# Order of the head of a hybrid decoder layer: constants and x first, gate2's sum around tile 1's first norm, its projection during the first routing, output weights scaled between slots

## The reference

```python
mod = silu(c) @ w_ada + b_ada
shift1, scale1, gate1, shift2, scale2, gate2 = split(mod, 6)
h = rms_norm(x, g_norm1) * (1 + scale1) + shift1
a, u, v = split(h @ w_in)                       # 512 columns each
mixed = concat([pool_mixer(a, w_pool, pool_scale), spatial_gating(u, v, ...)])
x = x + gate1 * (mixed @ w_out)
h = rms_norm(x, g_norm2) * (1 + scale2) + shift2
# for each token and head: two sets of 128 scores, top 16 of each, top 16 of the 256 sums
q = (h @ w_query).reshape(T, 8, 2, 128); scores = einsum(q, sub_keys)
idx, gate = top16 of the sums, softmax of their values
act = gelu(einsum('thkd,td->thk', expert_down[idx], h))
y = einsum('thk,thkd->td', gate * act, expert_up[idx])
return rms_norm(x + gate2 * y, g_final)
```

## Time and profile before

| | us |
|---|---|
| median of 3 runs | 2980.74 (2976.18 to 2981.69) |
| the profiled execution's own time | 2976.63 |
| its span, first to last instruction | 2974.8 |
| first gather issued | 158.9 |
| first expert sum on PE (slot 0) | 192.9 |
| DVE busy in the span | 1914.0 |
| PE busy in the span | 1978.3 |
| share of POOL's queue in the DMA engines' span | 88.2% |

### The profile page before, as it was taken

The page is one execution under the profiler, slowest core; times in us unless marked ns, Lnnn a source line. Parts: engine busy times, 40 slices in busy tenths (PEclk is TensorE's granted clock), DMA queues, the critical chain, the costliest instruction groups (busy, mean ns, idle before and its releaser), DMA issues.

```text
span 2974.8 us, 37539 instructions
## 1 busy us (share of the span) xinstructions
PE 1978.3 (67%) x12770; PEld 903.2 (30%) x12770; DVE 1914.0 (64%) x4705; ACT 1208.4 (41%) x3855; POOL 1150.8 (39%) x1032
## 2 busy tenths in 40 slices
PE   4579887887877466666656756666766666565553
PEld 3354452543543223222222322222322223222110
DVE  5666766576765476667576776667576766667544
ACT  1125454454453343444334443444334444344333
POOL 0033333334334244444444443444444444444332
PEclk9789987988988556675666556666566656666555
DMA  9469999999999999999999999999999999999997
GB/s 406 174 258 411 378 414 358 380 409 401 410 390 385 409 409 420 421 410 421 421 420 421 410 421 421 414 410 420 417 421 419 409 410 421 421 403 417 418 421 294
DMA packets 176213, 1181.83 MB, mean 397 GB/s; under 512 B 19731, under 2 KB 28947, under 8 KB 42774
## 3 DMA queue, kind: packets, MB, share of 16 engines
q0 software_dynamic: 147456, 1073.81, 88.2%
q1 hardware_dynamic: 28566, 105.63, 9.1%
HBM read 1170.98 MB, written 8.39 MB: 396 GB/s over the span
## 4 chain that ended last, share of the span: by engine, by line
DMA 54%; PE 23%; DVE 12%; ACT 6%; issue 3%; SPq 1%; POOL 0%; DVEq 0%; ACTq 0%; POOLq 0%
DMA work<-experts,expert_rows 39%; DMA weights<-experts,expert_rows 11%; PE ps_sum L746 7%; DVE work L1285 5%; PE ps_m L664 4%; PE ps_small L715 3%; PE ps_wide L690 2%; PE ps_m L608 2%; PE ps_m L628 2%; ACT diag L929 1%; ACT weight L924 1%; PE ps_m L619 1%; DMA out<-h_next 1%; DVE weights L1285 1%; DMA x_buf<-x 1%
## 5 line engine op out<-in xcount | busy, mean ns | idle before, releaser
L560 POOL DMA_INDIRECT work<-experts,expert_rows x832 | 928.3, 1116 | 1493.5 <-PE ps_sum L746 1311.7
L1285 DVE CUSTOM_DVE_ANT_0 work<-work 128x1024 f32<-128x1024 f32 x832 | 1015.0, 1222 | 658.0 <-DMA work<-experts,expert_rows 656.7
L746 PE MATMUL ps_sum<-work,diag 128*32 128x256 f32 x6656 | 745.4, 533 | 671.5 <-ACT diag L929 669.4
L922 ACT ACTIVATE act_out<-act_in 128x1 f32<-128x1 f32 x1024 | 207.4, 202 | 1206.7 <-DVE act_in L1285 1204.0
L746 PEld LDWEIGHTS ps_sum<-work,diag 128*32 128x32 f32 x6656 | 153.6, 127 | 1154.4 <-ACT diag L929 1086.0
L929 ACT ACTIVATE diag<-const,weight 128x32 f32<-128x32 f32 x1024 | 329.1, 321 | 33.5
L1285 DVE CUSTOM_DVE_ANT_0 weights<-weights,work 128x1024 f32<-128x1024 f32 x192 | 234.8, 1223 | 158.6 <-DMA weights<-experts,expert_rows 158.0
L560 POOL DMA_INDIRECT weights<-experts,expert_rows x192 | 219.5, 1143 | 299.2 <-PE ps_sum L746 281.1
L746 PE MATMUL ps_sum<-weights,diag 128*32 128x256 f32 x1536 | 182.5, 562 | 210.7 <-ACT diag L929 196.5
L924 ACT ACTIVATE weight<-gate,act_out 128x1 f32<-128x1 f32 x1024 | 301.7, 295 | 33.2
L690 PE MATMUL ps_wide<-h_cur,const 32*128 32x512 f32 x260 | 212.1, 907 | 0.8 <-ACT work L896 0.8
(11 more groups left out here) (159 smaller groups left out, 1712.5 us busy)
## 6 DMA issues: line engine op xcount, KB each, us to landing
work<-sides SPq DMA_DIRECT2D x68, 576.0 KB, 8.0
work<-w_ada SPq DMA_DIRECT2D x12, 2048.0 KB, 23.2
work<-experts,expert_rows POOLq DMA_INDIRECT x832, 16.2
weights<-sides SPq DMA_DIRECT2D x12, 576.0 KB, 31.6
weights<-w_in SPq DMA_DIRECT2D x3, 2048.0 KB, 16.9
x_buf<-x SPq DMA_DIRECT2D x8, 512.0 KB, 10.4
weights<-w_out SPq DMA_DIRECT2D x2, 2048.0 KB, 32.7
x_scratch<-h_buf SPq DMA_DIRECT2D x8, 512.0 KB, 7.0
```

Source lines behind the costliest of these rows:

```text
L560: nc.gpsimd.indirect_dma_start(ring[x.ring], None, experts, bass.IndirectOffsetOnAxis(ap=rows_flat[:, x.column:x.column + 1], axis=0),).th ...
L746: last = nc.tensor.matmul(ps_sum[quarter(c), x.group, :], diag[:, x.ring, :], ring[x.ring][:, D + c * QCOLS:D + (c + 1) * QCOLS], start=x. ...
L922: nc.scalar.activation(act_out[:, s:s + 1], act_in[:, s:s + 1], ACT.Gelu).then_inc(s_gelu, 1)
L1285: nc.vector.tensor_tensor_reduce(down, down, h2_spread[x.segment % 2], 1.0, 0.0, ALU.mult, ALU.add, act_in[:, x.g % TURN:x.g % TURN + 1]). ...
```

## The change

- SP issues the constants and x ahead of the first w_ada half; side (2, 1), the second of turn 2, is loaded from the loop instead of the head.
- DVE sums the first half of SHIFT1 ahead of FACTOR1 of tile 0. After `norm2(0)` it sums GATE2's first half, does FACTOR1 of tile 1, and sums the second half.
- ACT does ROOT1 of tile 1 ahead of the queries of turn 0, and SCALE_H of tile 1 after the first of them; COPY_H of tile 1 stands ahead of `exp_logits(0)`.
- PE does the projection V of tile 1 between GATE2's row sum and `move_choices(0)`. Only three sides of turn 1 stand in the head; the fourth is at slot 0.
- `MIX_HEAD` is 9 (PROJECT_A) instead of 13: the projection A, NORM_V, ROOT_V and SCALE_V of tile 1 are in slots 0 to 3, and each later step of tile 1 is 4 slots later (its residual at slot 25 instead of 21). Tiles 2 to 5 start 4 slots later, tile 6 three, tile 7 as before. Turn 1 is routed from slot 5 instead of 2.
- `scale_w_out` is four instructions of 128x2048 at slots 3, 6, 9 and 12 instead of two of 128x4096 in the head.

```diff
-MIX_HEAD = PROJECT_U
-MIX_AT = {1: -MIX_HEAD, 2: 25, 3: 64, 4: 103, 5: 142, 6: 181, 7: 220}
+MIX_HEAD = PROJECT_A
+MIX_AT = {1: -MIX_HEAD, 2: 29, 3: 68, 4: 107, 5: 146, 6: 184, 7: 220}
+
+SCALE_W_SLOTS = (3, 6, 9, 12)
...
-ROUTE_AT = [None, 2, 28, 50, 74, 98]
+ROUTE_AT = [None, 5, 28, 50, 74, 98]
...
-SIDE_AT = {(ROUTE_AT[e] - SIDES_BEFORE[b]): (e, b) for e in range(2, TURNS) for b in range(4)}
+SIDE_AT = {(ROUTE_AT[e] - SIDES_BEFORE[b]): (e, b) for e in range(1, TURNS) for b in range(4)
+           if ROUTE_AT[e] >= SIDES_BEFORE[b]}
...
+            sp.dma_start(const[:, :], constants).then_inc(s_const, 16)
+            load_x(0)
             load_ada(SHIFT1, 0)
-            load_x(0)
             load_ada(SHIFT1, 1)
-            sp.dma_start(const[:, :], constants).then_inc(s_const, 16)
...
-            for b in range(2):
-                load_side(2, b)
+            load_side(2, 0)
...
             mixer(TURN_H, 1)
             mod_rows(GATE2)
+            for n in range(TURN_H + 1, MIX_HEAD):
+                mixer(n, 1)
             move_choices(0)
-            for b in range(4):
+            for b in range(3):
                 side(1, b)
                 scores(1, b)
-            for n in range(TURN_H + 1, MIX_HEAD):
-                mixer(n, 1)
...
             copy_h2_t(0, 1)
+            mixer(ROOT1, 1)
             for b in range(4):
                 copy_query(0, b)
                 if b:
                     copy_score(0, b - 1)
+                else:
+                    mixer(SCALE_H, 1)
             copy_score(0, 3)
             copy_spread(0, 0)
             copy_spread(0, 1)
-            mixer(ROOT1, 1)
-            mixer(SCALE_H, 1)
+            for n in range(SCALE_H + 1, MIX_HEAD):
+                mixer(n, 1)
             exp_logits(0)
-            for b in range(4):
+            for b in range(3):
                 copy_query(1, b)
                 copy_score(1, b)
-            for n in range(SCALE_H + 1, MIX_HEAD):
-                mixer(n, 1)
...
+            sum_ada(SHIFT1, (0,))
             mixer(FACTOR1, 0)
-            sum_ada(SHIFT1)
+            sum_ada(SHIFT1, (1,))
...
             norm2(0)
+            sum_ada(GATE2, (0,))
             mixer(FACTOR1, 1)
-            sum_ada(GATE2)
+            sum_ada(GATE2, (1,))
             for n in range(ROUTE_STEPS):
                 route_step(n, 0)
             place_choices(0)
             gate2_rows()
-            scale_w_out(0)
-            scale_w_out(1)
-            mixer(NORM_V, 1)
-            mixer(SCALE_V, 1)
...
+                if x.g in SCALE_W_SLOTS:
+                    scale_w_out(SCALE_W_SLOTS.index(x.g))
```

More of the change, by code:

```diff
@@ L333, in build @@
         s_gain2 = sem("scale2_folded")
-        s_scaled_w = sem("w_out_halves_scaled")
+        s_scaled_w = sem("w_out_quarters_scaled")
         s_masked = sem("w_spatial_masked")
@@ L447, in load_x1_next @@
                 else:
-                    sp.wait_ge(s_scaled_w, 2)
+                    sp.wait_ge(s_scaled_w, len(SCALE_W_SLOTS))
                     sp.wait_ge(s_x1_gated, 1)
@@ L658, in mixer @@
                         if t == 1:
-                            pe.wait_ge(s_scaled_w, 2)
+                            pe.wait_ge(s_scaled_w, len(SCALE_W_SLOTS))
                     if n == PROJECT_OUT + 4:
@@ L1047, in scale_w_out @@
                 dve.wait_ge(s_mod, 2)
-                part = w_out_sb[:, 4 * n:4 * n + 4, :]
-                nc.vector.tensor_tensor(part, part, gate1[:, :].unsqueeze(1).to_broadcast([P, 4, D]),
+                part = w_out_sb[:, 2 * n:2 * n + 2, :]
+                nc.vector.tensor_tensor(part, part, gate1[:, :].unsqueeze(1).to_broadcast([P, 2, D]),
                                         ALU.mult).then_inc(s_scaled_w, 1)
```

## The result

The median of five runs is 2995.1 us (2991.22 to 2999.01), against 2980.74 (2976.18 to 2983.09) for five runs of the kernel before: a ratio of 1.0048, with a 95% interval of 1.0034 to 1.0063. The change makes the kernel **slower by 14.4 us**. I had forecast 2954, 22 sooner than the profiled execution of before, with a range of 2943 to 2970: the sign is wrong.

A forecast was written before the change was run, and what follows sets the result against it. The main loop was taken to run at its gathers' rate, with time lost ahead of it. The terms -26.3 (stage up to slot 26) and +4 (turn 1's choices) gave -22.3 from 2976.6, forecast 2954 us, range 2943 to 2970.

The forecast's parts named there:

- The rest: Loop: one more ACT table load, mixers 2 to 6 later, side (2, 1) loaded later; 0, mixers' bounds -5 and +5.
- rival B: Near slots 218 to 220: x of tile 7 comes late, ACT stands up to 10.8 us; 2965, chance 0.09.
- rival D: Loop behind the head: later mixers open new holes of 22 us that eat the gain; 2976, chance 0.06.
- GATE2's sum around FACTOR1: Head: with ROOT1 ahead of the queries, turn 0's routing starts at 126.0 instead of 140.7; -14.7 us.
- Constants and x first: Start of head: nothing gained, PE's longer wait lowers its clock; +2.6 us, bounds 0 and 2.6.
- Three sides instead of four: End of head, A in the loop: first expert sum near 159.8, gather 6 near 160.7, 33.1 us sooner.
- scale_w_out in quarters: Slots 3 to 12: POOL's long issues of gathers 1 and 2 go, quarters' holds are covered; 0, upper bound 8.8.
- The stage up to slot 26: Gathers 6 to 32: PE view 28.0 us sooner, bytes view 26.3; the smaller taken, -26.3 us.
- Turn 1's choices at slot 29: Slots 29 and 30: gather 32 waits for the later placing, late by 2.5 to 6.3 us; +4 taken.
- signs of being wrong: GATE1's load before 50, expert sum beyond 165, DMA share under 0.95, PEclk under 0.8, ACT idle over 5 us near slot 220.
- Rival C: Slots 0 to 26: PE's pauses drop TensorE's clock to its lower level, +13.9 us at a half; 2990, chance 0.05.

The follow-up runs named there:

- experiment 1: Kernel before with only the changed kernel's later MIX_AT (mixer starts) for tiles 2 to 6: 3010.93 us, ratio 1.0094.
- experiment 8: Experiment 2's kernel plus constants and x loaded first and SHIFT1's halves summed around FACTOR1: 2961.41 us, ratio 0.9921 against the kernel before.
- experiment 9: Experiment 2's kernel with w_out's four scaling quarters back in the head, ahead of v's norm: 2961.27 us, ratio 0.9934 against the kernel before.
- experiment 10: Experiment 2's kernel with projections V and A of tile 1 back behind turn 1's four sides: 2972.72 us, ratio 0.9976 against the kernel before.
- experiment 2: Kernel before with the head's new order and w_out quarters in the loop; loads, four sides, MIX_AT and ROUTE_AT as before: 2960.14 us, ratio 0.9915.
- experiment 11: Experiment 2's kernel with tile 0's add and the steps behind it four slots later in tile 1: 2956.42 us, ratio 0.9918 against the kernel before.
- experiment 7: Changed kernel with turn 1's choices moved at slot 23 and placed at 24, instead of 29 and 30: 2994.65 us, ratio 1.0046 against the kernel before.
- experiment 5: Changed kernel with tile 0's add and the steps behind it four slots later in tile 1: 2976.94 us, ratio 0.9984 against the kernel before.

## Why the prediction was wrong

**"The rest": the step that failed.** I wrote of the mixers' later starts "I take 0, bounds -5 and +5". Measured, they cost 30.2 us alone (experiment 1), and 31.3 in the change (from -16.7 at gather 120 to +14.6 at the last). The term of the sum was not only missized: the waits for loads that it stands for were left out. I had seen one of the four places, rival B, and gave it 10.8 us: ACT waited 10.0, and the stream lost 9.2. That the rows in the ring would cover most of it was wrong, since DVE's dots stop with ACT. I had also named the case that later mixers open holes and eat the gain, rival D, but with a chance of 0.06 and no place. The place could be read beforehand, and the price too: in the kernel before, ACT's wait of 4.3 for x of tile 4 has POOL standing for 7.6 us ahead of gather 110 (506.64). The row of the add already showed a wait of 4.4 us, so every slot taken from the reload had to show (four slots fewer, 8.6 us more of waiting); and SP's order of x and the output store changes with two numbers, 141 against 140. I moved the mixer's steps in mind, but not the fixed steps of the tile before, whose buffer they share. That is what decides the sign.

**"GATE2's sum around FACTOR1": right.** The routing starts at 124.9 (forecast 126.0 and up to 2.6 later); the first gather is at 143.0, 15.8 sooner instead of 12.1:

```profile
124.90 0.87 DVE L1194 MAX8 top_s<-wide 128x8 f32<-128x128 f32 x4 [4.23 <-ACT wide L911]
```

**"Constants and x first": no gain, as said, and the +2.6 was too much.** PE waits 8.9 us for v's norm, its clock falls as I feared (0.50 from 62.9 to 64.8), 8 matmuls of the spatial product take 2.07 instead of 1.16, and the 48 behind them 6.18 instead of 5.5: some 1.6 us in all, for a forecast of 2.6. The output projection then starts 1.15 later than before (76.75 for 75.60) and ends 0.4 sooner; experiment 8 finds nothing in the time.

```profile
62.90 2.07 PE L640 MATMUL ps_m<-w_sp_t,vn_u 128*128 128x128 f32 x8 [8.89 <-DVE vn_u L1139]
64.77 6.18 PE L630 MATMUL ps_m<-h_t,weights 128*128 128x128 f32 x48
```

**"Three sides instead of four": nearly.** Gather 6 is at 163.02, forecast 160.7. The third side waited 4.9 for its load (L717).

```profile
154.42 3.75 PE L717 MATMUL ps_small<-h_t,work 128*128 128x128 f32 x16 [4.92 <-DMA work<-sides]
```

**"scale_w_out in quarters" at 0: right in size.** While DVE scaled, POOL's issues were two to five times as long, and again in experiment 9; with no scaling beside them gathers 1 and 2 now start 1.39 and 1.24 us after the one before. The Trainium skill, SBUF — State Buffer (SBUF: two separate sides), has this exclusion, and the traces agree. By the rule alone, taking the hold away from 159.7 looks like a gain, but experiment 9 shows that moving the quarters into the loop is worth nothing measurable here. The 0 is a balance and not an absence: the quarters in the head cost 9.5 us at gather 6, and those in the loop cost part of the lead behind it (experiments 9 and 10).

**"The stage up to slot 26": the size was off.** I forecast 26.3 sooner; gather 31, which slot 25 frees, is 18.4 sooner. The fourth side, now beside slot 0, is late for the routing of turn 1, and DVE, which also does the dots, stands 11 us for it:

```profile
178.44 0.87 DVE L1194 MAX8 top_s<-wide 128x8 f32<-128x128 f32 x4 [10.98 <-ACT wide L911]
```

I counted the side as work for PE and left out who waits for it. How much of the missing 7.9 us this wait makes is not shown: with all four sides in the head gather 31 is 25.9 sooner in experiment 2, but 18.4 in experiment 8. Beyond this, a large lead at gather 6 is not kept: 29.8 and 27.9 (experiments 2 and 11) are 19.9 and 21.4 by gather 64, and the change's 30.8 is 11.5. The stream doesn't simply level all leads to the same 20, as I took it in the expectation of experiment 10: there 15.6 falls to 6.6, while the 20.3 of experiment 9, without quarters in the loop, stays 20.1. The rest of the cause is open. Of the signs of being wrong, the one for this stage came true: the DMA share from 165 to 235 was 0.91, and I had named 0.95 as the limit.

**"Turn 1's choices at slot 29": +4 counted, nothing lasting found.** POOL idles 12.7 us ahead of gather 32, because the placing comes so late: it stands behind the dot of slot 30, as I had written, and then behind FACTOR1 of tile 2, which waits 2.0 for ROOT1, which waits for x of tile 2. The second wait I had left out.

```profile
253.49 1.06 ACT L840 ACTIVATE h_buf<-x_buf 128x1024 f32<-128x1024 f32 x1 [2.03 <-DMA x_buf<-x]
```

```profile
256.27 0.16 DVE L1125 RECIPROCAL stat<-stat 128x1 f32<-128x1 f32 x1 [2.02 <-ACT stat L842]
256.35 0.17 DVE L1280 CAST expert_rows<-ps_wide 128x32 uint32<-128x32 f32 x1
```

```profile
256.80 0.94 POOL L562 DMA_INDIRECT work<-experts,expert_rows  x1 [12.67 <-DVE expert_rows L1280]
```

The lead is back at gather 40, with the hole (-16.4) or without it (-15.9, experiment 7). The term should have been 0. What bounds gather 40 instead was not looked for.

**Rival C, the clock:** nothing points to it. From 175 to 238 the granted clock was 1.00 and 0.93 in the windows above, and over the whole span it is 0.695, before 0.697. It was lower from 238 to 265 (0.75, before 0.94), where PE was busy for 16.6 of 27 us and the gathers stood for the placing, a hole that was worth nothing. At three of the four places where the lead is lost ACT stands for x, at the other DVE for the reload.

By steps: forecast -22.3, -16.4 measured at gather 40 and -16.7 at 120, then +31.3 where the forecast had 0.

## What to carry to other kernels

Where steps are moved against fixed ones, list for each load in flight the slot that lets it be issued and the slot that needs it, before and after: a distance that shrinks from six slots to two, or a load that falls behind a store on the same queue, can cost its whole wait, while its engine shows an unsuspicious share of busy time. A wait that is small now (4.4 us here) marks the place where the next shift will be paid. Check what a lead at one place is worth further on before it is counted: here 30 us at gather 6 were 20 at gather 64, and a hole of 12.7 us at gather 32 was worth nothing, but the 8.3 that went with a wait of 13 us of DVE's at slot 131 stayed lost to the end.

## What was unexpected of the hardware

A load of x that took 4.1 to 16.0 us from issue to landing took up to 22.9 to its use when it stood behind four output stores and a store of the residual on SP's queue, beside a full stream of gathers; in experiment 1 it was 21.0 in the same place. In experiment 5, where the same load is issued ahead of the output stores, it was 14.4 (603.51 to 617.86). That the stores made the difference is likely from this and not shown: the stream of gathers beside them was not the same.

TensorE's granted clock could not be guessed from one wait. In the changed kernel PE stood 8.9 us ahead of the spatial product, and the granted clock was 0.50 from 62.9 to 64.8. Yet the output projection behind it was faster than before, 15.49 us for 17.07:

```profile
76.75 15.49 PE L666 MATMUL ps_m<-weights,h_buf 128*128 128x512 f32 x32 [0.71 <-DVE h_buf L1157]
```

```profile
75.60 17.07 PE L664 MATMUL ps_m<-weights,h_buf 128*128 128x512 f32 x32 [0.71 <-DVE h_buf L1154]
```

Both began at the lower level. The granted clock was 0.50 from 76.75 to 79.5 in the changed kernel, and from 75.6 to 80.6 before; it reached 1.00 from 80.5 on and from 82 on. It is not shown that the early wait spared the slow stretch: experiment 2's kernel, in which PE waited only 0.24 us for the spatial product, needed the same 15.49 us, and that of experiment 8, in which it waited 7.6, needed 14.00.
